# A diffusion trunk step: the edge between sub-layers worked by column halves, and the FFN's first gated product ahead of its seventh split

## What is computed

```python
def ffn_sublayer(x, shift, scale, gate, g_pre, g_post, w_in, w_out):
    h = modulate(rmsnorm(x, g_pre), shift, scale)
    a, b = jnp.split(h @ w_in, 2, axis=-1)
    h = (jax.nn.silu(a) * b) @ w_out
    return x + FFN_RES * gate * rmsnorm(h, g_post)
```

## Time and profile before

| | |
|---|---|
| median of three executions | 3242.24 us |
| profiled execution | 3243.08 us, of which the span shown by the trace is 3241.2 |
| TensorE (PE) busy | 3075.8 us, 95% |
| VectorE (DVE), ScalarE (ACT), GpSimd (POOL) busy | 2152.7, 1141.7, 573.8 us |
| mean granted TensorE clock | 0.974 of full speed |

### The profile page before, as it was taken

The page is one execution under the profiler, slowest core; times in us unless marked ns, Lnnn a source line. Parts: engine busy times, 40 slices in busy tenths (PEclk is TensorE's granted clock), DMA queues, the critical chain, the costliest instruction groups (busy, mean ns, idle before and its releaser), DMA issues. The chain is left out here.

```text
span 3241.2 us, 48953 instructions
## 1 busy us (share of the span) xinstructions
PE 3075.8 (95%) x19650; PEld 2835.7 (87%) x19650; DVE 2152.7 (66%) x2879; ACT 1141.7 (35%) x1941; POOL 573.8 (18%) x578
## 2 busy tenths in 40 slices
PE   6999989999999999999999998679999999989999
PEld 5999878998999998998999997468998999878998
DVE  4777577777876657777875635647777877585444
ACT  3222454224322424224322533224224322554222
POOL 1112102112111112112111103642112112101001
PEclk8999999999999999999999998679999999999999
DMA  7667406665765445665665443025664766413443
GB/s 261 211 195 216 147 27 190 208 197 156 221 196 151 128 137 184 206 195 156 221 198 149 128 130 97 15 62 164 199 208 146 229 209 194 138 32 114 127 126 95
DMA packets 565511, 515.81 MB, mean 159 GB/s; under 512 B 42965, under 2 KB 499238, under 8 KB 563494
## 3 DMA queue, kind: packets, MB, share of 16 engines
q1 hardware_dynamic: 565286, 512.68, 51.6%
HBM read 509.37 MB, written 3.24 MB: 158 GB/s over the span
## 5 line engine op out<-in xcount | busy, mean ns | idle before, releaser
L1373 PE MATMUL bank<-h_hi,w_hi 128*128 128x384 f32 x3328 | 1115.7, 335 | 7.6 <-DVE tmp L1839 7.6
L1375 PE MATMUL bank<-h_hi,w_lo 128*128 128x384 f32 x3328 | 1113.5, 335 | 0.0
L1374 PE MATMUL bank<-h_lo,w_hi 128*128 128x384 f32 x3328 | 1112.9, 334 | 0.0
L1795 DVE TENSOR_TENSOR w_lo<-raw,w_hi 128x1024 fp32r<-128x1024 f32 x648 | 805.0, 1268 | 385.7 <-ACT w_hi L1636 380.7
L1636 ACT ACTIVATE w_hi<-raw 128x1024 fp32r<-128x1024 f32 x648 | 679.3, 1059 | 988.0 <-PE bank L1406 464.5
L1373 PEld LDWEIGHTS bank<-h_hi,w_hi 128*128 128x128 f32 x3328 | 624.8, 188 | 16.4 <-DVE tmp L1839 9.8
L1817 DVE SCALAR_TENSOR_TENSOR fold<-ada_raw,cond,fold 128x1024 f32<-128x1024 f32 x462 | 638.5, 1439 | 0.0
L1374 PEld LDWEIGHTS bank<-h_lo,w_hi 128*128 128x128 f32 x3328 | 624.8, 188 | 5.9
L1375 PEld LDWEIGHTS bank<-h_hi,w_lo 128*128 128x128 f32 x3328 | 624.6, 188 | 0.0
L2111 POOL TENSOR_TENSOR h_lo<-tmp,h_hi 128x384 fp32r<-128x384 f32 x176 | 284.9, 1619 | 1791.4 <-DVE h_hi L1843 1791.4
L1402 PE MATMUL bank<-w_hi,h_hi 128*128 128x512 f32 x1056 | 334.2, 397 | 0.0
(11 more groups left out here) (202 smaller groups left out, 2458.2 us busy)
## 6 DMA issues: line engine op xcount, KB each, us to landing
raw<-w_ffn_in SPq DMA_DIRECT2D x352, 512.0 KB, 5.0
ada_raw<-w_ada SPq DMA_DIRECT2D x272, 512.0 KB, 4.2
raw<-w_ffn_out SPq DMA_DIRECT2D x176, 512.0 KB, 4.7
raw<-w_hgrn_in SPq DMA_DIRECT2D x40, 512.0 KB, 5.0
g_rows<-g_dram SPq DMA_DIRECT2D x12, 1024.0 KB, 6.7
raw<-w_attn_qkv SPq DMA_DIRECT2D x24, 512.0 KB, 5.6
raw<-w_conv_in SPq DMA_DIRECT2D x24, 512.0 KB, 4.7
ada_first<-w_ada SPq DMA_DIRECT2D x16, 512.0 KB, 10.6
```

The source lines that it names most:

```text
L1373: mm(out, wh, h_hi[:, k, :], start=(k == 0), stop=False)
L1374: mm(out, wh, h_lo[:, k, :], start=False, stop=False)
L1375: last = mm(out, wl, h_hi[:, k, :], start=False, stop=(k == DC - 1))
L1795: V.tensor_tensor(w_lo[:, b % RING, :], raw[:, b % RAW, :], w_hi[:, b % RING, :].bitcast(F32), ALU.subtract).then_inc(w_lo_made, 1)
```

## The change

Three things. The tail's products, and those of all outward blocks, are ordered by banks: all products of a tile's left bank, then those of its right one; `acc_done` now signals each bank. ScalarE's, VectorE's and GpSimd's programs for the edge follow the halves. And VectorE's first gated product of an FFN stands ahead of its seventh split. The unread products go to bank 7 and are counted anew.

```diff
+        def out_half(b, t, n, hi, lo, opens, closes):
+            out = psum[2 * t + n][:, :]
+            mm(out, hi[:, tokens(t)], w_hi[:, b % RING, columns(n)], start=opens, stop=False)
+            mm(out, hi[:, tokens(t)], w_lo[:, b % RING, columns(n)], start=False, stop=False)
+            return mm(out, lo[:, tokens(t)], w_hi[:, b % RING, columns(n)], start=False, stop=closes)
...
             for t in range(NT):
-                for n, c in enumerate(chunks):
...
-                    last = out_tile(b + n, t, hi, lo, False, n == TAIL - 1)
...
-                if t < NT - 1:
-                    last.then_inc(acc_done, 1)
+                for n in range(2):
+                    for i, c in enumerate(chunks):
...
+                        last = out_half(b + i, t, n, hi, lo, False, i == TAIL - 1)
+                        if t == NT - 1 and n == 1:
+                            last.then_inc(block_done, 1)
+                        if t == NT - 1 and n == 0 and i == 0 and e < N_SUB:
                             turn_normed(e, 0)
+                    if t < NT - 1 or n == 0:
+                        last.then_inc(acc_done, 1)
             if e < N_SUB:
                 turn_normed(e, 1)
...
                     fold_up(late_fold(s), 6)
+                    unread_products(10)
                     ada_turn(late_fold(s), 7)
-                    unread_products(8)
...
-                    unread_products(16)
+                    unread_products(18)
                 turn_normed(e, 2)
-                unread_products(4)
                 if late_fold(s) is not None:
                     pe.wait_ge(mods_made, late_fold(s) + 1)
+                unread_products(1)
...
+                out_squares(e, 0, 0)
+                out_squares(e, 0, 1)
+                y_squares(e, 0)
+                out_squares(e, 1, 0)
+                out_squares(e, 1, 1)
+                modulate(e, 0, 0)
+                y_squares(e, 1)
+                out_squares(e, 2, 0)
+                modulate(e, 0, 1)
+                out_squares(e, 2, 1)
+                modulate(e, 1, 0)
+                y_squares(e, 2)
+                if late_fold(e - 1) is not None:
+                    ada_copy(2 * late_fold(e - 1), 6)
+                modulate(e, 1, 1)
+                modulate(e, 2, 1)
+                modulate(e, 2, 0)
...
             for f in range(FC):
-                for b in range(split_to, at_a(f) + 7):
-                    split(b0 + b)
-                split_to = max(split_to, at_a(f) + 7)
+                if f > 0:
+                    for b in range(split_to, at_a(f) + 7):
+                        split(b0 + b)
+                    split_to = max(split_to, at_a(f) + 7)
...
+        def gated(e, t, n):
...
+            dve.wait_ge(squares_made, square_number(e, t, n, False) + 1)
+            V.tensor_tensor(og[:, t % 2, columns(n)], psum[2 * t + n][:, :], g_rows[:, group_of(t), columns(n)],
+                            ALU.mult).then_inc(og_made, 1)
...
-                gp.wait_ge(h_high_made, 2 * NT * e + 4)
+                gp.wait_ge(hn_made, 2 * NT * (e + 1))
```

More of the change, by code:

```diff
@@ L1446, in unread_products @@
             for _ in range(n):
[L1447 removed]
+                mm(psum[7][:, 0:P], ident, ones[:, :], start=True, stop=True)
         def out_tail(s, chunks, b):
@@ L1452, in out_tail @@
             for t in range(NT):
-                for n, c in enumerate(chunks):
[L1454 to L1457, removed]
-                    last = out_tile(b + n, t, hi, lo, False, n == TAIL - 1)
-                    if t == NT - 1:
-                        last.then_inc(block_done, 1)
-                        if n == 0 and e < N_SUB:
+                for n in range(2):
+                    for i, c in enumerate(chunks):
+                        if t == 0 and n == 0:
+                            pe.wait_ge(w_lo_made, b + i + 1)
+                            out_ready(s, c)
+                        hi, lo = moving_out(s, c)
+                        last = out_half(b + i, t, n, hi, lo, False, i == TAIL - 1)
+                        if t == NT - 1 and n == 1:
+                            last.then_inc(block_done, 1)
+                        if t == NT - 1 and n == 0 and i == 0 and e < N_SUB:
                             turn_normed(e, 0)
-                if t < NT - 1:
-                    last.then_inc(acc_done, 1)
+                    if t < NT - 1 or n == 0:
+                        last.then_inc(acc_done, 1)
             if e < N_SUB:
@@ L1688, in mixer, with out_squares @@
                 split(b0 + n_in + c)
-        def out_squares(e, t):
+        def out_squares(e, t, n):
             s = e - 1
-            if t < NT - 1:
-                act.wait_ge(acc_done, (NT - 1) * s + t + 1)
+            if t < NT - 1 or n == 0:
+                act.wait_ge(acc_done, acc_number(s, t, n))
             else:
                 act.wait_ge(block_done, first_block[e])
[L1697 to L1703, removed]
+            number = square_number(e, t, n, False)
+            act.wait_ge(squares_made, number - 2)
+            A(junk[number % 3], psum[2 * t + n][:, :], ACT.Square, scale=1.0 / 32,
+              accum_out=o_ss[:, 2 * t + n:2 * t + n + 1]).then_inc(squares_made, 1)
         def y_squares(e, t):
@@ L1729, in boundary @@
         def boundary(e):
[L1730 to L1741, removed]
-                    y_squares_after(e, 2)
-                    modulate(e, 1, 0)
-                    modulate(e, 1, 1)
-                    modulate(e, 2, 1)
-                    modulate(e, 2, 0)
+            if e == N_SUB:
+                for t in range(NT):
+                    out_squares(e, t, 0)
+                    out_squares(e, t, 1)
+            elif e > 0:
+                out_squares(e, 0, 0)
[15 more added lines that the diff above has]
+                modulate(e, 2, 0)
             else:
@@ L1979, in boundary @@
                 y_variance(e, 1)
-                gated(e, 2, (1,))
                 normed(e, 1)
-                gated(e, 2, (0,))
+                gated(e, 2, 0)
+                hi_of(e, 0, 1)
                 out_variance(e, 2)
+                gated(e, 2, 1)
                 residual(e, 2)
-                hi_of(e, 0, 1)
+                hi_of(e, 1, 0)
                 y_variance(e, 2)
@@ L1989, in boundary @@
                     mod_add(late_fold(e - 1), 7)
-                hi_of(e, 1, 0)
+                hi_last(e, 0)
                 hi_of(e, 1, 1)
-                hi_last(e, 0)
                 hi_last(e, 1)
@@ L1997, in boundary @@
                 for t in range(NT):
-                    gated(e, t, (1, 0))
+                    gated(e, t, 0)
                     out_variance(e, t)
+                    gated(e, t, 1)
                     residual(e, t)
```

34 lines of the change are left out of this document (8 added, 26 removed).

## The result

The changed kernel takes 3217.74 us (median of 4 runs, 3217.09 to 3219.92) against 3242.01 us of the kernel before beside it: ratio 0.9926, 95% interval 0.9913 to 0.9938. It is faster by 24.3 us, or 0.74%. The prediction said 3213.3, faster by 28.9; the time lies inside its range. 4.6 us of the forecast gain are missing.

A forecast was written before the change was run, and what follows sets the result against it. TensorE was taken to bound the kernel, leaving only its waits at sub-layer edges to gain: 18.7 (11 edges x 1.7) + 9.5 (FFN) + 0.7 (last edge) = 28.9 us, giving 3213.3 us, range 3206 to 3226.

The forecast's parts named there:

- The chain behind the tail: At each edge, variance 0.91 us behind the tail's end (was 2.19), third transposes (turn 2) 5.47 behind (was 6.75).
- Turn 0 late by 0.56 to 0.7: First transposes inside the tail wait 0.56 us for hn, taken as 0.7, behind tile 1's gated product.
- The rival of a turn 0 that isn't late: First transposes in the tail not late, calmer neighbours: 11 x 0.7 us more gain, 3205.6; chance 0.08.
- So 23.42: Third transposes (turn 2) at each edge come 23.42 us after the tail's start, a gain of 0.58.
- 1.1 us from turn 2 to the first product: At each edge, hi_last ahead of hi_of starts the next sub-layer's first product 0.7 + 0.78 us after the third transposes.
- GpSimd early, hidden by 0.2: At each edge GpSimd's h_lo operations start once hn is complete; VectorE's h_lo ends 0.2 us before TensorE wants it.
- Rival (a): SBUF hand-over between GpSimd and VectorE at edges goes wrong: up to 1.1 us each, 3225; at worst 3235; chance 0.18.
- FFN 9.5: In seven FFNs the first gated product ahead of the seventh split removes TensorE's stall: 9.5 us.
- Rival (b): In the FFN, the stall moves to the second gated product instead of going: 9.5 us lost, 3223; chance 0.08.
- rival (e): Out blocks' bank order costs time per product: 7.7 ns eats the whole gain, 5 ns gives 3232; chance 0.03.
- Last edge 0.7: Behind the last tail, the residual comes 1.66 us after the last block's signal instead of 2.39: gain 0.7.
- Rival (d), the clock: TensorE gaps at edges bring the lower clock, 3.4 us each, 37 us over 11 edges: 3251; chance 0.03.

The follow-up runs named there:

- the mended kernel: Changed kernel with the tail's tile 0 chunk by chunk, and VectorE's variance and normed of tile 0 ahead of tile 1's gated product: 3206.46 us.
- guard: Kernel before with only the split of the FFN's seventh block put behind the first gated product: 3233.24 us, 9.8 less.
- the two moves: Kernel before with VectorE's hi_last(0) ahead of hi_of(1,1) and GpSimd waiting on tile 2's hn, no halves: 3231.55 us; 9.4 gained by the marks.

## Why the prediction was right, and where it was off

- **The chain behind the tail**, 0.91 to the variance and 5.47 to turn 2: 0.92 and 5.49. Right.
- **Turn 0 late by 0.56 to 0.7** because a gated product was put ahead of its variance: right at ten edges (0.61 to 0.63 by the run without that product; 0.98 at the first attention's), and taking it away gave 0.7 back. The rival of a turn 0 that isn't late (3205.6) is the mended kernel (3206.5), which also has the other defect mended.
- **"So 23.42": the step that was mis-sized.** Turn 2 was to come 0.58 earlier at eleven edges. It did at three (0.6), and at the others it came 0.06 (seven) and 0.24 (one) earlier. The step took the tail as 72 products without a wait, read from a conv tail, where `o_hi` and `o_lo` had long been made. Halves also change the order in which a tail asks for its chunks, and behind an FFN the last chunk's `h2_lo` comes after product 9 and is late: 0.49 in each of eight FFN tails, 3.9 us of the missing 4.6. Behind the first attention the loss is 0.37. It stays in the run with the old order of tile 0 and is gone in the one with VectorE's mended order, so it is part of turn 0's wait. The rows place it but do not explain it: ScalarE's read-out ends at 495.85 and VectorE's gated product of tile 1 starts 0.45 later, with no other instruction named, where at the conv edge it is 0.10 (1218.55 to 1218.65).

```profile
495.66 0.19 ACT L1701 ACTIVATION_READ_ACCUMULATOR tmp<-bank 128x1 f32 x1
496.30 0.69 DVE L1889 TENSOR_TENSOR og<-bank,g_rows 128x512 f32<-128x512 f32 x1 [1.78 <-ACT tmp L1701]
```

- **1.1 us from turn 2 to the first product**: 1.48 measured, as forecast (0.7 + 0.78). The reason was half right. VectorE's order gives it on the kernel before (0.85, the rest under keep-busy products), but on the changed kernel it is not needed.
- **GpSimd early, hidden by 0.2**: hidden by 0.38, with the collision where it was forecast. Rival (a), a worse hand-over, did not occur. The prediction did not say what the early start was worth; without it 1.4 us an edge are lost.
- **FFN 9.5**: 9.8. Rival (b) fell; the seventh split had the room.
- **Bank order 0**: the pitch is 0.227 in both kernels, and rival (e) fell.
- **Last edge 0.7**: VectorE's variance stands 0.91 behind the last product, its residual 0.94 later, both as forecast. The last tail, an FFN's, takes 0.50 more for the late `h2_lo`, so 0.2 are left of the 0.7:

```profile
3210.38 0.21 DVE L1881 TENSOR_SCALAR small<-small 128x1 f32<-128x1 f32 x1 [1.96 <-ACT tmp L1701]
...
3211.32 1.42 DVE L1902 SCALAR_TENSOR_TENSOR y<-og,small,y 128x512 f32<-128x512 f32 x2
```

- **Rival (d), the clock**, did not occur in the changed kernel, whose longest wait at the edge shown is 0.46. But it was the right thing to fear: one call at another place on ScalarE brings it on. Its price was set too high: where the clock fell it cost 1.2 to 1.6 us an edge, not 3.4.

The account of the change by the marks: guard 9.8, the two moves 9.4, fewer keep-busy products 2.9, halves 2.3, last edge 0.7 less the 0.5 of its tail, together 24.6, against 24.3 measured.

## What to carry to other kernels

When a loop nest over blocks and halves is turned round, write down for every operand after how many products it is now asked for, and compare that with when it is made, in each kind of stage and not in the one that was walked through. In an in-order queue, look at every instruction put ahead of the critical chain for what it waits for itself: here one such product cost 0.7 us at most edges, and one such copy costs 1.8 us and the clock as soon as its producer on another engine moves. Two moves that only pay together (an order, and a start that no longer asks for what was moved back) are measured together; each alone can read as nothing or as a loss.

## What the runs showed of the hardware

- A wait that the trace prints as 0.20 us of TensorE idle cost 0.45: the start-to-start was 0.37 longer at the waiting product and 0.08 at the next. Small waits are better read as start-to-start than as idle.
- A gap of 2.2 to 2.5 us ahead of the transposes, with keep-busy products ahead of it, brought the granted clock down to 0.50 at eight edges of eleven and not at the other three, in each of two kernels' profiled executions, and not at the same eight; gaps of 0.3 to 0.8 us at the same place did not in the profiled execution of any kernel here.
- VectorE's copy of 128x512 took 0.42 us by itself and 1.25 inside a GpSimd operation. Four GpSimd operations beside VectorE took 5.21 to 5.93 us, by when they started.
